# Two weight slots, a chunk slot and a new order of copies at the out-projection of a hybrid encoder layer

## The reference

```python
mod = silu(c) @ w_ada[l] + b_ada[l]
sh_a, sc_a, g_a, sh_m, sc_m, g_m = split(mod, 6)
h = rms_norm(x, norm_mix[l]) * (1.0 + sc_a) + sh_a
p = h @ w_in[l]
...                                    # o_mla, o_sb, o_fx: three groups of heads
o = concatenate([head_rms_norm(o_mla, g_mla), head_rms_norm(o_sb, g_sb), head_rms_norm(o_fx, g_fx)])
x = x + g_a * (o @ w_out[l])
h = rms_norm(x, norm_ffn[l]) * (1.0 + sc_m) + sh_m
x = x + g_m * (square(relu(h @ w_ff1[l])) @ w_ff2[l])
```

## Time and profile before

| | |
|---|---|
| median of three runs | 1165.99 us (1168.31, 1135.22, 1165.99) |
| the profiled execution: time, span | 1139.96 us, 1138.2 us |
| TensorE busy | 1100.8 us, 97% |
| VectorE, ScalarE, GpSimd busy | 720.1, 532.7, 315.3 us |
| mean granted TensorE clock | 0.988 |
| moved by DMA | 296.88 MB |

### The profile page before, as it was taken

How to read it: one execution, slowest core, us unless ns; L and a number is a source line. 1 busy time by engine, 2 the same in 40 slices (tenths; PEclk the granted TensorE clock), 3 DMA queues, 4 the chain that set the end, 5 groups by cost and what they waited for, 6 DMA issues and landing times.

```text
span 1138.2 us, 21704 instructions
## 1 busy us (share of the span) xinstructions
PE 1100.8 (97%) x9084; PEld 1067.6 (94%) x9084; DVE 720.1 (63%) x924; ACT 532.7 (47%) x674; POOL 315.3 (28%) x157
## 2 busy tenths in 40 slices
PE   7889999999998999999999999999999999999996
PEld 6779999997798989999999999999999999999995
DVE  4588868788865569877776444545555555445453
ACT  4644454676563344544544434343544444344441
POOL 3997997866048960000000000000000000000001
PEclk9999999999999999999999999999999999999998
DMA  9999999998659977888786665666666666656651
GB/s 362 408 390 398 395 375 368 366 361 298 232 187 383 342 285 278 301 305 288 273 280 200 190 199 189 197 193 199 188 195 195 196 189 195 199 190 193 195 184 74
DMA packets 81888, 296.88 MB, mean 261 GB/s; under 512 B 9088, under 2 KB 9216, under 8 KB 81792
## 3 DMA queue, kind: packets, MB, share of 16 engines
q1 hardware_dynamic: 81792, 295.50, 73.6%
HBM read 293.37 MB, written 2.10 MB: 260 GB/s over the span
## 4 chain that ended last, share of the span: by engine, by line
PE 81%; DMA 6%; DVE 3%; POOL 3%; ACT 3%; issue 3%; SPq 0%; DVEq 0%; ACTq 0%
PE ps L1402 48%; PE ps L1408 24%; DMA ada<-in_ada 4%; PE ps L1420 3%; POOL w_lo L840 2%; PE ps L1589 2%; DMA raw<-in_weights 1%; PE ps L1425 1%; DVE ada L965 1%; ACT w_hi L486 1%; PE ps L1599 0%; POOL ssq L834 0%; ACT o_tok L747 0%; PE ps L1555 0%; PE ps L1554 0%
## 5 line engine op out<-in xcount | busy, mean ns | idle before, releaser
L486 ACT ACTIVATE w_hi<-raw 128x1024 fp32r<-128x1024 f32 x346 | 363.4, 1060 | 440.2 <-PE ps L1408 357.8
L946 DVE TENSOR_TENSOR w_lo<-raw,w_hi 128x1024 fp32r<-128x1024 f32 x254 | 308.8, 1224 | 267.1 <-ACT w_hi L486 266.7
L1402 PE MATMUL ps<-hT,w_hi 128*128 128x256 f32 x3072 | 381.7, 277 | 9.4 <-ACT w_hi L486 3.2
L1402 PEld LDWEIGHTS ps<-hT,w_hi 128*128 128x128 f32 x3072 | 364.3, 188 | 12.7 <-issue 6.4
L1402 PE MATMUL ps<-act,w_hi 128*128 128x256 f32 x2048 | 252.9, 276 | 0.0
L1402 PEld LDWEIGHTS ps<-act,w_hi 128*128 128x128 f32 x2048 | 241.6, 188 | 0.0
L840 POOL TENSOR_TENSOR w_lo<-raw,w_hi 128x1024 fp32r<-128x1024 f32 x92 | 219.7, 2408 | 55.0 <-ACT w_hi L486 54.7
L1408 PE MATMUL ps<-hT,w_lo 128*128 128x256 f32 x1536 | 206.6, 277 | 0.9 <-DVE w_lo L946 0.6
L834 POOL TENSOR_TENSOR ssq<-ssq,sq 128x1024 f32<-128x1024 f32 x6 | 14.4, 2401 | 657.3 <-ACT sq L493 657.3
L1408 PEld LDWEIGHTS ps<-hT,w_lo 128*128 128x128 f32 x1536 | 189.4, 188 | 1.3 <-DVE w_lo L946 0.8
L1408 PE MATMUL ps<-act,w_lo 128*128 128x256 f32 x1024 | 136.9, 276 | 0.0
(11 more groups left out here) (228 smaller groups left out, 821.2 us busy)
## 6 DMA issues: line engine op xcount, KB each, us to landing
raw<-in_weights SPq DMA_DIRECT2D x346, 512.0 KB, 4.3
ada<-in_ada SPq DMA_DIRECT2D x180, 512.0 KB, 6.2
more<-in_weights SPq DMA_DIRECT2D x16, 512.0 KB, 8.6
more<-in_ada SPq DMA_DIRECT2D x12, 512.0 KB, 8.5
xT<-in_xt SPq DMA_DIRECT2D x4, 512.0 KB, 7.0
y<-tmp SPq DMA_DIRECT2D x4, 256.0 KB, 2.5
consts<-in_consts SPq DMA_DIRECT2D x1, 580.0 KB, 12.7
y<-sq SPq DMA_DIRECT2D x2, 256.0 KB, 3.0
```

What stands on the lines that cost most here:

```text
L486: sc.activation(w_hi[:, slot, :, :], raw_room(u0 + j), ACT.Copy).then_inc(hi_done, 1)
L946: ve.tensor_tensor(w_lo[:, slot, :, :], raw_room(u), w_hi[:, slot, :, :].bitcast(F32), ALU.subtract).then_inc(lo_vec, 1)
L1402: pe.matmul(acc[:, n, :], w, rhs[:, kt0 + k, half, :], start=first and k == 0 and n % 2 == 0 and half == 0, stop=False, skip_group_check=True)
```

## The change

- Six raw slots (two of them in `more`) serve units 78 to 101, and five ada slots (one in `more`) tiles 128 to 147. Loads into `more` wait for the latents' last unit: `unit_used` at B_OUT. Two tables (`uses_of`) replace the formulas for a slot's earlier use and its round. `past`, 768 bytes per partition, keeps `ssq` off the end of `more`.
- SyncE's due times: units 78 and 79 directly behind attention step 9; units up to 101 as soon as the unit six earlier is used; tiles 128 to 132 at the start of the out-projection, and from 133 on one per unit, beginning at T_OUT + 4.6.
- ScalarE, after the steps: the copy of unit 79 first, then the square, then out_hi(2) and out_hi(3), the copy of unit 80, and all 16 scalings in one piece, with unit 81's copy behind them.
- VectorE: the last sum and head_mean ahead of out_lo(2) and out_lo(3); five tiles (128 to 132) ahead of out_lo(4), and none between out_lo(5) and out_lo(6). Then one tile per unit from j = 3 on; tiles below 143 stand ahead of gate_out(0).
- GpSimd: before the copy of unit 79 it waits for `head_scaled` 3.

```diff
--- before.py
+++ after.py
@@ -70,6 +70,8 @@
 WIDE, RAWS = 5, 6
 A_WIDE = A_GA - A_GA % WIDE
 U_WIDE = 48
+A_LATE, A_LATE_END = A_OUT, A_OUT + 20
+U_LATE, U_LATE_END = B_OUT + RING, B_OUT + RING + 24
 MIX_POOL = {10: 1, 16: 2, 19: 3}
 
 
@@ -94,32 +96,32 @@
 
 def ada_slot(a):
 
-    return a % WIDE if a < A_WIDE else (a - A_WIDE) % ADA
-
-
-def ada_round(a):
-
-    return a // WIDE + 1 if a < A_WIDE else A_WIDE // WIDE + (a - A_WIDE) // ADA + 1
-
-
-def ada_before(a):
-
-    return a - WIDE if a < A_WIDE + ADA else a - ADA
+    if A_WIDE <= a < A_LATE or a >= A_LATE_END:
+        return (a - A_WIDE) % ADA
+    return a % WIDE if a < A_WIDE else (a - A_LATE - 1) % WIDE
 
 
 def raw_slot(u):
 
-    return u % RAWS if u < U_WIDE else u % RING
-
-
-def raw_before(u):
-
-    return u - RAWS if u < U_WIDE + RING else u - RING
-
-
-def raw_round(u):
-
-    return u // RAWS + 1 if u < U_WIDE else U_WIDE // RAWS + (u - U_WIDE) // RING + 1
+    if U_WIDE <= u < U_LATE or u >= U_LATE_END:
+        return u % RING
+    return u % RAWS if u < U_WIDE else (4, 5, 2, 3, 0, 1)[(u - U_LATE) % RAWS]
+
+
+def uses_of(slot_of, count):
+
+    last, rounds, before, number = {}, {}, [], []
+    for n in range(count):
+        slot = slot_of(n)
+        before.append(last.get(slot, -1))
+        last[slot] = n
+        rounds[slot] = rounds.get(slot, 0) + 1
+        number.append(rounds[slot])
+    return before, number
+
+
+ADA_BEFORE, ADA_ROUND = uses_of(ada_slot, A_END)
+RAW_BEFORE, RAW_ROUND = uses_of(raw_slot, UNITS)
 
 
 ADA_STOPS = ((8, 9, 10, 12, 14, 16, 17, 18, 19), (19, 21, 23, 25, 27, 30, 32, 32, 32),
@@ -176,7 +178,7 @@
 
 def ada_out(j):
 
-    at = lambda i: A_OUT + 4 + (A_GM - A_OUT - 4) * min(24, max(0, i - 5)) // 24
+    at = lambda i: A_OUT + 5 + (A_GM - A_OUT - 5) * min(26, max(0, i - 3)) // 26
     return range(at(j), at(j + 1))
 
 
@@ -245,6 +247,7 @@
                 el = sb("el", [P, 2, 3 * P], F32, v)
                 sp = sb("sp", [P, 2, 3 * P], F32, v)
         act = sb("act", [P, HALF, 2, S], F32R)
+        past = sb("past", [P, 192])
         ssq = sb("ssq", [P, 4, S])
         sq = sb("sq", [P, 4, S])
         squares = (tmp, tmp2, sq, qk[:, 0:4, :])
@@ -384,15 +387,15 @@
             units = list(range(U_IN))
             units += [U_IN + 2 * t for t in range(7) for _ in LAT_OF[t]]
             units += [T_OUT + j for j in range(U_OUT + AHEAD)]
-            due = [(units[max(0, u - RING)] + SHIFT, 0, u) for u in range(B_FF + AHEAD)]
+            due = [(units[max(0, u - RING)] + SHIFT if not U_LATE <= u < U_LATE_END else
+                    max(U_IN + 2 * H + 2, units[u - RAWS] + SHIFT), 0, u) for u in range(B_FF + AHEAD)]
             for p, n in enumerate(PARTS):
                 for b in range(BLOCKS):
                     due += [(8 * PART_AT[p] + n * b, 1, a) for a in ada_in_part(p, b)]
             for t in range(STEPS):
                 due += [(U_IN + 2 * t if t < H else U_IN + 2 * H + 1.2 * (t - H), 1, a) for a in ada_at(t)]
-            due += [(T_OUT + m, 1, A_OUT + m) for m in range(4)]
-            for j in range(U_OUT):
-                due += [(T_OUT + 2 + j, 1, a) for a in ada_out(j)]
+            due += [(T_OUT + m, 1, A_OUT + m) for m in range(WIDE)]
+            due += [(T_OUT + LAG + 0.6 + m, 1, A_OUT + WIDE + m) for m in range(A_GM - A_OUT - WIDE)]
             due += [(T_OUT + 2 + U_OUT + 2 * m, 1, A_GM + m) for m in range(ADA)]
             return [(kind, n) for _, kind, n in sorted(due)]
 
@@ -433,14 +436,18 @@
         @block.sync
         def _(sp):
             def load_unit(u):
-                if u >= RAWS:
-                    sp.wait_ge(*lo_ready(raw_before(u)))
+                if RAW_BEFORE[u] >= 0:
+                    sp.wait_ge(*lo_ready(RAW_BEFORE[u]))
+                if U_LATE <= u < U_LATE_END and raw_slot(u) >= RING:
+                    sp.wait_ge(unit_used, B_OUT)
                 sp.dma_start(raw_room(u).rearrange("p k n -> p (k n)"),
                              weights[u, :, :]).then_inc(raw_full[raw_slot(u)], 16)
 
             def load_ada(a):
-                if a >= WIDE:
-                    sp.wait_ge(ada_done, ada_before(a) + 1)
+                if ADA_BEFORE[a] >= 0:
+                    sp.wait_ge(ada_done, ADA_BEFORE[a] + 1)
+                if a == A_LATE:
+                    sp.wait_ge(unit_used, B_OUT)
                 sp.dma_start(ada_room(a), w_ada[a, :, :]).then_inc(ada_full[ada_slot(a)], 16)
 
             sp.dma_start(cols[:, :], cols_in).then_inc(ld_cols, 16)
@@ -480,7 +487,7 @@
         def _(sc):
             def hi(u0, step, it, j):
                 slot = (u0 + j) % RING
-                sc.wait_ge(raw_full[raw_slot(u0 + j)], 16 * raw_round(u0 + j) + (16 * step // RING) * it)
+                sc.wait_ge(raw_full[raw_slot(u0 + j)], 16 * RAW_ROUND[u0 + j] + (16 * step // RING) * it)
                 if u0 + j >= RING:
                     sc.wait_ge(unit_used, u0 + j - RING + 1 + step * it)
                 sc.activation(w_hi[:, slot, :, :], raw_room(u0 + j), ACT.Copy).then_inc(hi_done, 1)
@@ -748,21 +755,19 @@
                 if n % 2 == 1:
                     ins.then_inc(normed_mla, 1)
 
+            hi(B_OUT + LAG, 0, 0, 1)
+            square_outputs(3)
             out_hi(2)
-            square_outputs(3)
             out_hi(3)
-            hi(B_OUT + LAG, 0, 0, 1)
+            hi(B_OUT + LAG, 0, 0, 2)
             head_rough(2, AT_ML, H)
             sc.wait_ge(c_kept, 2)
             sc.wait_ge(op_lo, R_O + 4)
             sc.activation(crep_ps[1], c_rep[:, D // 2:D], ACT.Copy).then_inc(c_back, 1)
             sc.wait_ge(head_scaled, 3)
-            for n in range(4):
+            for n in range(H):
                 norm_mla(n)
-            hi(B_OUT + LAG, 0, 0, 2)
             hi(B_OUT + LAG, 0, 0, 3)
-            for n in range(4, H):
-                norm_mla(n)
             out_hi(4)
             out_hi(5)
             hi(B_OUT + LAG, 0, 0, 4)
@@ -921,6 +926,8 @@
                                      ALU.mult).then_inc(normed, 1)
 
             for j in range(U_OUT - LAG + 2):
+                if j == 1:
+                    gp.wait_ge(head_scaled, 3)
                 lo(B_OUT + LAG + j)
                 if j == 8:
                     gp.memset(ssq[:, :, :], 0.0).then_inc(zeroed, 1)
@@ -959,7 +966,7 @@
                     part, c = half_sum[:, a % 2:a % 2 + 1], crep_ps[half] if a < A_GA else c_rep[:, half * D // 2:(half + 1) * D // 2]
                 bias = cols[:, C_B + KT * g + kt:C_B + KT * g + kt + 1] if g not in (SC_A, SC_M) else \
                     plus_one[:, kt:kt + 1] if g == SC_A else plus_one[:, KT + kt:KT + kt + 1]
-                ve.wait_ge(ada_full[ada_slot(a)], 16 * ada_round(a))
+                ve.wait_ge(ada_full[ada_slot(a)], 16 * ADA_ROUND[a])
                 if a >= 2:
                     ve.wait_ge(ada_done, a - 1)
                 ve.tensor_tensor_reduce(out=room, in0=room, scale=1.0,
@@ -1277,18 +1284,17 @@
                 if t == H + 17:
                     sum_outputs(2)
             read_group(7)
-            out_lo(2)
             sum_outputs(3)
-            out_lo(3)
             ve.wait_ge(out_summed, 4)
             head_mean(8, AT_ML, H, VD).then_inc(head_step, 1)
+            out_lo(2)
+            out_lo(3)
             head_newton(9, AT_ML, H)
             ve.wait_ge(c_back, 1)
-            for a in range(A_OUT, A_OUT + 3):
+            for a in range(A_OUT, A_OUT + WIDE):
                 ada_tile(a)
             out_lo(4)
             out_lo(5)
-            ada_tile(A_OUT + 3)
             out_lo(6)
             out_lo(7)
```

## The result

The changed kernel's median is 1132.42 us (20 runs), that of the kernel before 1139.92 us (20 runs). The ratio of the two is 0.9946, with a 95% interval of 0.9933 to 0.9959: 6.1 us faster (4.7 to 7.6), 0.5% of the time. Some executions of either kernel take some 27 us longer, 5 of the 20 before and 3 of the 20 after; the ratio leaves them out, but two of the three times shown beforehand were of this kind. The profiled execution of the changed kernel took 1133.37 us, its span 1131.6 against 1138.2.

What follows compares the result with a forecast made beforehand. TensorE, busy 97% of the span, bounds the kernel, so only its waits and their clock loss can be won: 1.56 + 6.23 + 0.95 = 8.7 us off 1165.99 gives 1157 us, range 1124 to 1164.

Steps and rivals of the forecast that it cites:

- The turns: TensorE's wait before the last two turns of the heads goes, as the norm in one piece ends earlier: 1.56 us gained.
- the hole at block 2: TensorE's 3.16 us wait before out-projection block 2, with its clock loss, goes as loads restart earlier: 6.23 us gained.
- Part 1's transfers in attention: Extra slots let loads leave earlier, between 262 and 315 us; they cost nothing there, up to 1 us at worst.
- this sign of being wrong: Attention's tiles waiting for DMA would show the forecast wrong; no such VectorE wait was seen between 262 and 315 us.
- The end of the stage: At the final sum, gate_out(3) starts at TensorE's end, no longer behind the last tile and gain: 0.95 us gained.
- The base of the number: Whole-kernel time the gain is taken from: 1165.99 us, as two of three timed runs stood at the upper level.
- The hole shrinks but stays: Rival, chance 0.25: shared bandwidth leaves a wait at block 2, gain 4.7 to 7.7 us, median 1158 to 1161.
- The gate comes later: Rival, chance 0.08: GpSimd's copies pace SP's loads, so gate_out(0) is later than before; 3.6 us slower, 1169.6.
- only the turns are won: Rival, chance 0.10: the wait before block 2 moves with TensorE; gain 0 to 1.6 us, 1164 to 1166.
- The clock: Rival, chance 0.07: the upper level comes from clock lost after holes; median falls to 1127, 3.4% faster.

Runs made afterwards that it cites:

- room alone: Changed kernel with the old order on ScalarE, VectorE and GpSimd around the last heads, new slots and due times kept; ratio 0.9958 to the kernel before.
- norm alone: Kernel before with only the new order of the last heads' norm and GpSimd's wait, slots and due times as before; ratio 0.9989 to the kernel before.
- gate first: Kernel before with gate_out(0) behind tile 136 in VectorE's order instead of tile 140; ratio 0.9992 to the kernel before.
- without GpSimd's wait: Changed kernel with GpSimd's wait for head_scaled 3 removed; ratio 0.9986 to the kernel before.
- all columns: Changed kernel with every column of the MLP's gain made by itself, scalar operand, behind its tile; ratio 0.9948 to the kernel before.

## Why the prediction came out as it did

**The turns** (1.56 us forecast, 1.35 measured) and **the hole at block 2** (6.23 forecast, 6.24 measured): right in place, mechanism and size. The restart of the loads came at 330.05 (forecast 330.9), and the DMA ran at 383 to 417 GB/s from 335 to 370. Counted from the first out-projection unit tile 142 was at the late edge of its bounds, and the margin was 0.55 us: that no hole was left was near. The Trainium skill, "SBUF — State Buffer", section "A bandwidth-pool intuition that's wrong (but worth ruling out)", gives about 358 GB/s from HBM to a core. By this figure a hole of 1.4 us would have been left by my estimate; none was, and the traffic stood above the figure, so here the measurement decides. That room and norm were both needed was in my sum, and the runs don't bear it out: room alone closes the hole, norm alone leaves 2.04 us.

**Part 1's transfers in attention**: VectorE now waits 0.8 us in two waits for tiles between 262 and 315 us, where it had no such wait, so this sign of being wrong came true in small. The stretch from the latents' last unit to the first of the out-projection was longer by 0.3 us, and by none in the second trace, within the 0 to 1 us given. The prediction called 4.0 us VectorE's largest wait there; by the earlier trace rows it is the sum of six, and the longest is 1.4.

**The end of the stage** is the step of the sum that failed. It forecast 0.95 us gained, and 2.17 us were lost in the first trace, 0.47 in the second. Two things were wrong in it. (1) It took the loads up to tile 159 as one full queue with some 3 us added, so landed by 404 at the latest; VectorE starts the tile at 405.60. SyncE's order had stood still from 379.2 to 385.7, where the slots fall back from six to four. (2) It left the gain's product at the price of the trace before, 0.77 us, and it took 2.35 and 1.85. The prediction had seen that head_mean took 2.22 us and ended exactly with a GpSimd copy, and did not look for other instructions that might be held like it. The 2.17 us are 1.72 of hole more than before, and 0.45 of the granted clock, 0.66 of full from 410 to 415. The six matmuls behind these eight were slower too (2.74 us, 1.46 before), but that only filled TensorE's wait for rstd, which fell from 1.57 to 0.33 us.

**The base of the number** is the second step that failed, and the one that put the forecast of 1157 some 25 us off. It took 1165.99, the median of the three times shown, as the kernel's usual time, and by 20 runs that is 1139.92. The step rested on two runs of three. From the profiled execution, 1139.96, the same sum gave 1131.3, and that kernel's was 1133.4: 8.7 us forecast, 6.1 in the runs, 6.6 in the spans, of which the stage has 5.5 (7.4 by the second trace). The range of 1124 to 1164 holds the measured time only because it was drawn over both bases.

**The rivals.** "The hole shrinks but stays" came true only in the kernel with the norm alone. "The gate comes later" and "only the turns are won" did not occur. "The clock" expected some 39 us back; the runs gave 6.1, so it did not occur. A rival that should have been there: the room's end, the place where more slots become fewer.

## What to carry to other kernels

When a stall goes, walk the chain of the next one with the same suspicion: the same form of instruction, the same queue, the last load. Where GpSimd copies without a pause, keep VectorE's instructions with two SBUF operands out of that stretch, or make them single columns with a scalar operand, or make GpSimd wait. Look at each place where a pool of slots shrinks: the first load there waits for the younger copy and holds everything behind it. And before you take a median of three as the base, compare it with the profiled execution.

## What the runs showed of the hardware

**A VectorE instruction with two SBUF operands is held by GpSimd's copies, sometimes across several.** head_mean's step took 0.17 us alone and 2.2 us at one copy; the gain's product took 5.1, 5.5 and 14.0 us in rows of copies that follow directly, and passed two, two and five places where one ended and the next began. Each held instruction ended within 0.1 us of the end of some copy. But it needn't be the last of the row. In the kernel before the product was let in at such a place (VectorE's product, GpSimd's copies):

```profile
415.55 0.77 DVE L991 TENSOR_TENSOR gain<-mod,cols 128x16 f32<-128x16 f32 x1
```

```profile
413.92 2.38 POOL L840 TENSOR_TENSOR w_lo<-raw,w_hi 128x1024 fp32r<-128x1024 f32 x1
416.25 2.36 POOL L840 TENSOR_TENSOR w_lo<-raw,w_hi 128x1024 fp32r<-128x1024 f32 x1
```

It was the same with gate first (1.28 us), with the norm only (1.57 us) and for head_mean's first step without GpSimd's wait (1.45 us, above). So the theory in the expectation of "all columns", that such an instruction waits for a pause of GpSimd, holds in five traces and fails in four. What decides between the two isn't shown. The Trainium skill, "SBUF — State Buffer", section "Who interferes with whom", says that whichever starts first holds the shared pair for the whole instruction and the other blocks. The traces agree on the blocking; that the other can stay blocked when the next copy follows at once is beyond what the section says.

**TensorE has a slightly slower pace at full granted clock.** In the kernel with room only, units in order of time, and a stretch (busy times, granted clock, DMA share, GB/s):

```profile
351.31 2.05 PE L1410 MATMUL ps<-hT,w_hi 128*128 128x256 f32 x16
...
354.14 2.05 PE L1410 MATMUL ps<-hT,w_hi 128*128 128x256 f32 x16
```

```profile
345.00:365.00 20.00, 20.00 (x172) 20.00 (x172) 12.91 (x23) 7.31 (x7) 19.32 (x9) 1.00 1.01 392
```

A unit's groups take 2.05 and 1.10 us here where the other traces have 1.98 and 1.07 in this stage. It holds from 340 to 410 us, in a stage that no hole interrupted, and a unit takes 2.72 us again soon behind the pause of the final sum. DMA ran at 392 GB/s, and the changed kernel had 405 in the same stretch at 1.98 us. The pace doesn't belong to this kernel's order, as the changed kernel has it too, in its input projection:

```profile
203.97 2.05 PE L1408 MATMUL ps<-hT,w_hi 128*128 128x256 f32 x16
```

There this trace has 8 units of 2.83 us and the changed kernel's second trace 39. At 0.11 us each that is up to 3.4 of the 5.9 us by which the second trace comes later to the out-projection, by my estimate, so the pace can be a part of why that mark differs from trace to trace. What starts it isn't settled.
